# Out-norm of three head groups ahead of the last pages, an LRU gate without reciprocal, and part of the SSD on GpSimd

## The reference

```python
def rms_norm(x, g):
    y = x * lax.rsqrt(jnp.mean(x * x, axis=-1, keepdims=True) + EPS)
    return y * g

# RG-LRU
a = jnp.exp(log_a)
bterm = jnp.sqrt(-jnp.expm1(2.0 * log_a)) * (i * xb)
# SSD, carried states
h = chunk_decay * h + states
# mixer output, heads of 64
y = jnp.concatenate([y_ssd, y_lru, y_hgrn2, y_mla], axis=-1).reshape(b, L, 16, 64)
y = rms_norm(y, out_norm.reshape(16, 64)).reshape(b, L, 1024)
x = x + g2 * (y @ w_out)
```

## Time and profile before

| | |
|---|---|
| runs | 1904.53, 1911.35, 1911.89 us; median 1911.35 |
| profiled execution | 1913.51 us, span 1911.8 us, mean granted clock 0.944 |
| busy (share of the span) | PE 1771.8 (93%), DVE 957.6 (50%), ACT 610.9 (32%), POOL 237.4 (12%) |
| chain that ended last | PE 80%, DVE 14%, ACT 3%, DMA 1% |

### The profile page before, as it was taken

The page is one execution under the profiler, slowest core; times in us unless marked ns, Lnnn a source line. Parts: engine busy times, 40 slices in busy tenths (PEclk is TensorE's granted clock), DMA queues, the critical chain, the costliest instruction groups (busy, mean ns, idle before and its releaser), DMA issues.

```text
span 1911.8 us, 28829 instructions
## 1 busy us (share of the span) xinstructions
PE 1771.8 (93%) x11864; PEld 1524.4 (80%) x11864; DVE 957.6 (50%) x1729; ACT 610.9 (32%) x972; POOL 237.4 (12%) x434
## 2 busy tenths in 40 slices
PE   4999999999989788999989999999998887899998
PEld 3999996667667556999979999967766664699998
DVE  3544432465775644354445444236767745444443
ACT  2433321033231324343334333111433233333331
POOL 8000003510044000000000000072003210000000
PEclk8999999999887889999999999999998788999999
DMA  9566647862011253554453544493201123435542
GB/s 316 192 198 202 207 144 227 272 213 84 1 53 42 101 186 116 166 182 131 162 172 130 178 135 159 149 255 106 93 25 35 38 67 132 132 133 176 169 145 67
DMA packets 206275, 272.06 MB, mean 142 GB/s; under 512 B 11778, under 2 KB 182238, under 8 KB 206144
## 3 DMA queue, kind: packets, MB, share of 16 engines
q1 hardware_dynamic: 188240, 236.90, 37.9%
q0 software_dynamic: 17904, 33.33, 6.1%
...
## 4 chain that ended last, share of the span: by engine, by line
PE 80%; DVE 14%; ACT 3%; DMA 1%; issue 1%; SPq 0%; DVEq 0%; ACTq 0%
PE bank L782 16%; PE bank L784 16%; PE bank L783 16%; PE bank L913 10%; PE bank L1048 4%; PE bank L1309 4%; PE bank L719 2%; DVE sq L2269 2%; PE bank L1221 1%; PE bank L709 1%; DMA ring<-in_w_ada_dram 1%; DVE big L1995 1%; PE bank L1021 1%; PE bank L1191 1%; DVE zs L1628 1%
## 5 line engine op out<-in xcount | busy, mean ns | idle before, releaser
L784 PE MATMUL bank<-hT_r,ring_r 128*128 128x320 f32 x1408 | 440.5, 313 | 0.0
L784 PEld LDWEIGHTS bank<-hT_r,ring_r 128*128 128x128 f32 x1408 | 267.5, 190 | 0.0
L1636 DVE TENSOR_TENSOR ring_r<-ring,lat_pages_r 128x2048 fp32r<-128x2048 f32 (+1 forms) x68 | 151.4, 2229 | 162.4 <-ACT lat_pages_r L1335 162.4
L782 PE MATMUL bank<-hT_r,lat_pages_r 128*128 128x320 f32 x704 | 218.9, 311 | 13.5 <-DVE gates_r L1668 13.5
L783 PE MATMUL bank<-gates_r,lat_pages_r 128*128 128x320 f32 x704 | 219.3, 312 | 0.0
L784 PE MATMUL bank<-big_r,ring_r 128*128 128x320 f32 x704 | 218.0, 310 | 0.0
L913 PE MATMUL bank<-hT,ring 128*128 128x320 f32 x736 | 209.6, 443 | 4.7 <-DVE hT L1662 4.7
L913 PEld LDWEIGHTS bank<-hT,ring 128*128 128x128 f32 x736 | 140.9, 194 | 65.2 <-issue 11.6
L1335 ACT ACTIVATE lat_pages_r<-ring 128x2048 fp32r<-128x2048 f32 (+1 forms) x68 | 126.4, 1862 | 142.8 <-DMA ring<-in_w_ffn_in_dram 69.4
L782 PEld LDWEIGHTS bank<-hT_r,lat_pages_r 128*128 128x128 f32 x704 | 134.0, 190 | 19.0 <-issue 18.5
L783 PEld LDWEIGHTS bank<-gates_r,lat_pages_r 128*128 128x128 f32 x704 | 133.9, 190 | 0.0
...
## 6 DMA issues: line engine op xcount, KB each, us to landing
...
lat_pages<-in_cache_mla_latent_dram POOLq DMA_DIRECT2D x128, 64.0 KB, 2.2
...
```

The lines of the kernel that those rows point to most:

```text
L782: mm(out, w_h, x_h, start=start, stop=False)
L784: return mm(out, w_l, x_h, start=False, stop=stop)
L1636: go(v.tensor_tensor(slot_r(n, nk, 256), slot(n, nk, 256), w_hi_r[g % HI][:, 0:nk].bitcast(F32), ALU.subtract), w_low)
```

## The change

- The sum products of the out-norm go to bank 7 in halves (one chunk each), ScalarE takes the root straight from the bank (scale and epsilon inside it), and VectorE inverts the root and multiplies in one step, `scale`. `invert` and the semaphore `on_inv` go. `BATCH` puts MLA's prompt batch third, and batches 0 to 2 are squared, summed and scaled around `from_states` and `score(5)` instead of after it; batch 3 stands before `soft_exp(2)` on ScalarE and before `soft_values(2)` on VectorE. Dummy products go (14 before `turn(5)`, 20 before `soft_turn(2)`).
- The LRU takes sqrt((1 + a^2) t) in place of sqrt(2 t/(1 + t)): one square on ScalarE, one product on VectorE.
- GpSimd does `spread_b` and the decay of the SSD states, between its page loads. On VectorE `att_inv(0)` and `att_scores(0)` follow `turned_states(1)`; on TensorE `turn(1)` follows `new_states(0)`, with 8 dummy products after it in place of 12.

```diff
-BATCH = [(0, 0, T), (2, 0, T), (4, 0, T), (6, 0, TP), (6, TP, T)]
+BATCH = [(0, 0, T), (2, 0, T), (6, 0, TP), (4, 0, T), (6, TP, T)]
+BATCH_AT = [0, 640, 0, 1280, 640]
...
+        def norm_tmp(n):
+            _, c0, c1 = BATCH[n]
+            return carve(sq, BATCH_AT[n], 2, T)[:, :, c0:c1]
...
     store_latents(pool, l)
+    def spread_b(j):
+        pool.tensor_tensor(bm_blk[0:64], bm_tok[0:64, 2, j * P:(j + 1) * P].unsqueeze(1).to_broadcast([64, NB, P]),
+                           c("seqmask", 64).unsqueeze(2).to_broadcast([64, NB, P]), ALU.mult).then_inc(blk_ready, 1)
+    pool.wait_ge(rest_loaded, 16)
+    pool.wait_ge(ssd_dve, at(ssd_dve, 3))
+    spread_b(0)
+    pool.wait_ge(ssd_act, at(ssd_act, 3))
+    pool.wait_ge(ssd_pe, at(ssd_pe, 4))
+    for j in range(2):
+        ends = Es[:, j, P:].rearrange("p (b t) -> p b t", b=NB)[:, :, TS - 1]
+        pool.tensor_tensor(ssd_state[:, j], ssd_state[:, j], ends.unsqueeze(2).to_broadcast([P, NB, P]),
+                           ALU.mult).then_inc(decayed, 1)
+    pool.wait_ge(ssd_pe, at(ssd_pe, 5))
+    spread_b(1)
     pool.wait_ge(group_used, at(group_used, 1))
...
     keep_busy(8)
-    turn(1)
-    keep_busy(12)
     pe.wait_ge(ssd_dve, at(ssd_dve, 5))
 
     def new_states(j):
 
+        pe.wait_ge(blk_ready, at(blk_ready, j + 1))
         for q in range(2):
             ins = mm(bank[1 + q][:, :], xdt_end[0:64, 2, j * P:(j + 1) * P], bm_blk[0:64, 4 * q:4 * q + 4],
                      start=True, stop=True)
...
     for j in range(2):
         pe.transpose(bank[0][:, j * P:(j + 1) * P], hp[:, j], c("ident"))
     new_states(0).then_inc(ssd_pe, 1)
+    turn(1)
+    keep_busy(8)
     score(1)
...
+    def out_norm(n, half):
+        if half == 0:
+            pe.wait_ge(on_sq, at(on_sq, n + 1))
+        if n or half:
+            pe.wait_ge(on_root, at(on_root, 2 * n + half))
+        _, c0, c1 = BATCH[n]
+        mm(bank[7][:, c0:c1], c("ones64"), norm_tmp(n)[:, half], start=True, stop=True).then_inc(on_pe, 1)
...
     value_taken(1)
     turn(4)
     score(4)
-    keep_busy(14)
+    out_norm(0, 0)
     turn(5)
+    out_norm(0, 1)
     pe.wait_ge(hg_dve, at(hg_dve, 7))
     block_sums(2).then_inc(hg_pe, 1)
+    out_norm(1, 0)
     from_states(0, 0, 0).then_inc(hg_pe, 1)
+    out_norm(1, 1)
     from_states(1, 1, 0)
+    out_norm(2, 0)
     from_states(2, 1, 256).then_inc(hg_pe, 1)
+    out_norm(2, 1)
     score(5)
-    def out_norm(n):
-        pe.wait_ge(on_sq, at(on_sq, n + 1))
-        if n:
-            pe.wait_ge(on_inv, at(on_inv, n))
-        k0, c0, c1 = BATCH[n]
-        for k in range(k0, k0 + 2):
-            ins = mm(bank[2 + k % 2][:, c0:c1], c("ones64"), sqx[:, k, c0:c1], start=True, stop=True)
-        ins.then_inc(on_pe, 1)
 
     tail_tiles, tail_steps = iter(TAIL[l]), sorted({step for step, _ in TAIL[l]})
 
...
         if i < len(tail_steps):
             ada_turn(tail_steps[i])
 
-    keep_busy(20)
     soft_turn(2)
     soft_spread(2)
-    out_norm(0)
+    out_norm(3, 0)
     tail(1)
+    out_norm(3, 1)
     value(2)
     value_taken(2)
     turn(6)
-    out_norm(1)
-    tail(1)
+    tail(2)
     score(6)
     tail(2)
-    out_norm(2)
     turn(7)
     tail_turn(0)
     tail(1)
     score(7)
-    out_norm(3)
     tail(4)
     soft_turn(3)
     tail_turn(1)
...
     tail(1)
     value(3)
     value_taken(3)
+    pe.wait_ge(on_root, at(on_root, 8))
     for h in range(4):
         r = slice(64 * (h % 2), 64 * (h % 2) + 64)
         ins = mm(bank[7][r, (h // 2) * 64:(h // 2) * 64 + 64], wv[:, h * 64:(h + 1) * 64],
                  pn.rearrange("p b (h t) -> p b h t", h=4)[:, :, h], start=True, stop=True)
     ins.then_inc(mla_pe, 1)
     tail(3)
-    out_norm(4)
-    tail(2)
+    out_norm(4, 0)
+    tail(1)
+    out_norm(4, 1)
+    tail(1)
     tail_turn(2)
...
+    def on_square(n):
+        ac.wait_ge(mixed, at(mixed, n + 1))
+        k0, c0, c1 = BATCH[n]
+        if n == 2:
+            ac.wait_ge(on_scaled, at(on_scaled, 1))
+        o.go(f(norm_tmp(n), hT[:, k0:k0 + 2, c0:c1], ACT.Square), on_sq)
+    def on_sqrt(n):
+        _, c0, c1 = BATCH[n]
+        for half in range(2):
+            ac.wait_ge(on_pe, at(on_pe, 2 * n + half + 1))
+            o.go(f(norm_tmp(n)[:, half], bank[7][:, c0:c1], ACT.Sqrt, bias=eps, scale=1.0 / 64), on_root)
...
         o.go(f(la[:, j], lr[:, j], ACT.Exp, scale=lam8[:, j:j + 1]))
-        o.go(f(lt[:, j], lr[:, j], ACT.Tanh, scale=nlam8[:, j:j + 1]), lru_act)
+        o.go(f(lt[:, j], lr[:, j], ACT.Tanh, scale=nlam8[:, j:j + 1]))
+    o.settle()
+    o.go(f(lm, la, ACT.Square), lru_act)
     ac.wait_ge(lru_dve, at(lru_dve, 1))
-    o.go(f(lm, lm, ACT.Sqrt, scale=2.0), lru_act)
+    o.go(f(lm, lm, ACT.Sqrt), lru_act)
     att_copy(2)
     att_squares(2)
     att_root(2)
...
     att_root(3)
     soft_exp(1)
     att_copy(4)
+    on_square(0)
+    on_square(1)
     att_squares(4)
     att_root(4)
+    on_sqrt(0)
     att_copy(5)
+    on_sqrt(1)
+    on_square(2)
+    on_sqrt(2)
     att_squares(5)
     att_root(5)
-    def batch(x, n):
-        k0, c0, c1 = BATCH[n]
-        return x[:, k0:k0 + 2, c0:c1]
-    def on_square(n):
-        ac.wait_ge(mixed, at(mixed, n + 1))
-        o.go(f(batch(sqx, n), batch(hT, n), ACT.Square), on_sq)
-    def on_sqrt(n):
-        ac.wait_ge(on_inv, at(on_inv, n + 1))
-        o.go(f(batch(sqx, n), batch(sqx, n), ACT.Sqrt), on_root)
-    for n in range(4):
-        on_square(n)
+    on_square(3)
+    on_sqrt(3)
     soft_exp(2)
-    on_sqrt(0)
     att_copy(6)
-    on_sqrt(1)
     att_squares(6)
     att_root(6)
     tail_copy(0)
     att_copy(7)
-    on_sqrt(2)
     att_squares(7)
     att_root(7)
     tail_copy(1)
     soft_exp(3)
-    on_sqrt(3)
     on_square(4)
+    on_sqrt(4)
     tail_copy(2)
-    on_sqrt(4)
     tail_copy(3)
...
-    def spread_b(j):
-        go(v.tensor_tensor(bm_blk[0:64], bm_tok[0:64, 2, j * P:(j + 1) * P].unsqueeze(1).to_broadcast([64, NB, P]),
-                           bview(c("seqmask", 64), P), MUL))
-    spread_b(0)
     for cc, (t0, L) in enumerate(TC):
         ve.wait_ge(ssd_act, at(ssd_act, 4 + cc))
         if cc == 2:
...
     turned_states(0)
     o.settle()
-    att_inv(0)
-    att_scores(0)
     ve.wait_ge(ssd_pe, at(ssd_pe, 4))
     do(v.tensor_copy(hp, bank[3][:, 0:256].rearrange("p (j n) -> p j n", j=2)))
     for j in range(2):
         go(v.scalar_tensor_tensor(last_ssd[:, j], hp[:, j], Es[:, j, P - 1:P], bank[3][:, (2 + j) * P:(3 + j) * P], MUL, ADD))
-        ends = Es[:, j, P:].rearrange("p (b t) -> p b t", b=NB)[:, :, TS - 1]
-        go(v.tensor_tensor(ssd_state[:, j], ssd_state[:, j], bview(ends, P), MUL))
     turned_states(1)
     o.settle()
+    att_inv(0)
+    att_scores(0)
     hg_gates()
     ve.wait_ge(ssd_pe, at(ssd_pe, 5))
     go(v.tensor_copy(hpT, bank[0][:, 0:256].rearrange("p (j n) -> p j n", j=2)))
...
             s = ssd_state[:, j, 4 * q:4 * q + 4]
             go(v.tensor_tensor(s, s, bank[1 + q][:, :].rearrange("p (b n) -> p b n", b=4), ADD))
-    spread_b(1)
+    ve.wait_ge(decayed, at(decayed, 2))
     add_states(0)
     o.tell(ssd_dve)
     att_inv(1)
...
     soft_values(0)
-    ve.wait_ge(lru_act, at(lru_act, 2))
-    do(v.tensor_scalar(lm, lt, 1.0, None, ADD))
-    do(v.reciprocal(lm, lm))
-    do(v.tensor_tensor(lm, lm, lt, MUL), lru_dve)
+    ve.wait_ge(lru_act, at(lru_act, 1))
+    do(v.scalar_tensor_tensor(lm, lm, 1.0, lt, ADD, MUL), lru_dve)
...
-    go(v.tensor_tensor(hT[:, 2:4], lh, gelu, MUL))
+    do(v.tensor_tensor(hT[:, 2:4], lh, gelu, MUL))
+    for n in range(3):
+        o.tell(mixed)
     go(v.tensor_tensor(wf, wf, kh, MUL), hg_dve)
...
         w = hg_state[:, :, 4 * i:4 * i + 4]
         go(v.tensor_tensor(w, w, bank[2 + i].rearrange("p (j v b) -> p j b v", j=2, b=4), ADD))
     o.tell(out_ready)
+    def scale(n):
+        k0, c0, c1 = BATCH[n]
+        x = norm_tmp(n)
+        ve.wait_ge(on_root, at(on_root, 2 * n + 2))
+        do(v.reciprocal(x, x))
+        for k in range(k0, k0 + 2):
+            y = hT[:, k, c0:c1]
+            go(v.scalar_tensor_tensor(y, y, col("out_norm", k), x[:, k - k0], MUL, MUL), on_scaled if k > k0 else None)
+    scale(0)
+    scale(1)
     ve.wait_ge(hg_pe, at(hg_pe, 5))
     add_from_states(0, 0, 0)
     ve.wait_ge(hg_pe, at(hg_pe, 6))
...
     add_from_states(2, 1, 256)
     o.settle()
     do(v.tensor_tensor(hT[:, 4:6], oacc, gh, MUL))
-    for n in range(4):
-        o.tell(mixed)
+    o.tell(mixed)
+    scale(2)
     att_inv(5)
     att_scores(5)
     soft_max(2)
-    def invert(n):
-        k0, c0, c1 = BATCH[n]
-        ve.wait_ge(on_pe, at(on_pe, n + 1))
-        for k in range(k0, k0 + 2):
-            go(v.tensor_scalar(sqx[:, k, c0:c1], bank[2 + k % 2][:, c0:c1], 1.0 / 64, EPS, MUL, ADD))
-        o.settle()
-        go(v.reciprocal(sqx[:, k0:k0 + 2, c0:c1], sqx[:, k0:k0 + 2, c0:c1]), on_inv)
-    def scale(n):
-        k0, c0, c1 = BATCH[n]
-        ve.wait_ge(on_root, at(on_root, n + 1))
-        for k in range(k0, k0 + 2):
```

(24 more changed lines are left out.)

2 lines of the change are left out of this document (removed).

## The result

The changed kernel takes 1921.3 us (median of 7 runs, 1915.2 to 1931.5) against 1911.6 for the kernel before: a ratio of 1.0063 with the interval [1.0043, 1.0082], 12 us slower by the ratio, 10 by the medians. I had said "within 0.5%, 1907.3", with a range that ended at 1920. The profiled execution is a good one of its kernel: 1918.1 us, span 1916.4.

A forecast was written before the change was run, and what follows sets the result against it. Bound: mixer stages, by waits behind small steps, above all VectorE reciprocals, with TensorE's clock partly halved. Sum +0.3 - 3.6 + 9.2 - 7.3 - 2.6 = -4.0 us from 1911.35 gives 1907.3, within 0.5%; range 1893 to 1920.

The forecast's parts named there:

- my slower rival: Idling where 14 dummy products stood before turn 5 halves the clock: 5.3 us per layer there, 1923 in all; chance 0.16.
- +0.3: SSD stage, both layers: `score(1)` slightly earlier in layer 0 (-0.3), later in layer 1 (+0.6), GpSimd work free.
- I take 0, and +1 per layer at the upper end: SSD spread and decays on GpSimd: cost nothing on the path unless they outlast their cover.
- my 4.5 of cover: SSD decays on GpSimd: up to 4.5 us for each is hidden before VectorE asks for them.
- `score(1)` at 499.5: SSD stage, layer 0: page 1's scores start at 499.5 against 499.76, after turn 1 and 8 dummy products (1.8 us).
- +9.2 and -9.9: Out-norm, both layers: early sums at `from_states` cost 9.2 us; the tail gains 7.3 and 2.6.
- my 2.5: Tail, without the 20 dummy products before `soft_turn(2)`: TensorE idles, half clock costs 2.5 us a layer (none to 5).
- LRU -3.6: LRU without reciprocal: TensorE's waits before `score(2)`, 1.66 and 1.98 us, disappear; gain 3.6 us for both layers.
- The cap by dummy products: LRU: 28 dummy products (6.36 us) stand before `score(2)`, so anything gained beyond TensorE's remaining wait is hidden.
- From_states 4.6 a layer: Five halves of sum matmuls before `score(5)`: 2.9 us at full clock plus 1.7 for half clock, 4.6 per layer.
- as soon as the 8-column products fill the engine: `from_states`: clock granted at half from 614.1 on, so the last three sum halves double, +1.7 us.
- The tail: From `soft_spread(2)` on: +2.0 first, for roots and a 4.15 us reciprocal, then gains; -9.8 layer 0, -5.1 layer 1, before half-clock loss.

The follow-up runs named there:

- `lru_20`: LRU part alone on the kernel before, with 20 dummy products instead of 28 ahead of `score(2)`: 1907.0 us, ratio 0.9966.
- `no_ssd`: The changed kernel with the SSD part undone, leaving the LRU and out-norm parts: 1910.8 us, ratio 1.0011 to the kernel before.

## Why the prediction was wrong

The number of my slower rival, 1923 for "the wait before turn 5" (0.16 of the chance), is near the 1921.3 measured, but it is near by luck. It priced the SSD part at +0.3 us, and that part alone costs 9.6 by its ratio. It priced the loss from turn 5 on at 5.3 us a layer above my forecast, where the changed kernel's trace has 1.7 and 1.5. What it has right is the kind of loss, a lower clock once the dummy products are gone. Two terms of the sum failed, SSD and out-norm.

- **The SSD part, "+0.3"**, is where the trace itself contradicts the sum. "I take 0, and +1 per layer at the upper end" for GpSimd was wrong by 2.1 us a layer. I asked only whether GpSimd would be done in time. The decays were (1.89 us each, well inside my 4.5 of cover). The damage is the other way round: VectorE's copy waits for a GpSimd product nobody is waiting for yet. I had priced an operation's length and its reader, and not its neighbour on the other engine. With the spreads back on VectorE 4 us return by the ratios.
- **`score(1)` at 499.5** took the turn and 16 records of dummy products at full clock. After 3.71 us of idling the turn ran at half (1.97 us) and so did part or all of the dummy products: turn 1 to the scores took 4.5 us in layer 0 and 5.5 in layer 1 where I had 3.1. With the GpSimd term this is 8 of the 9.6 us that the SSD part costs.
- **The out-norm part, +9.2 and -9.9 = "-0.7"**, holds in the profiled execution (-1.3) and fails in the median (+8.4, by the ratio +10.5). The step that failed is the price of lower clock: the lost dummy products ahead of turn 5 at nothing and those ahead of `soft_turn(2)` at 2.5 us a layer, 5.0 in all. Ten and 20 of them put back give 8.4 by the ratios (4.8 by the medians). Taken out of the kernel before, they cost 11.1 together; alone the first cost 5.0 us a layer and the second 1.0 to 2.0, which its interval doesn't tell from my 2.5. I didn't believe the rival's 5.3 because the trace of before shows no fall at that place. It can't: it shows the clock with the dummy products in front. Where in the changed kernel the 8.4 us are lost stays open.
- **"LRU -3.6"** was right: -3.4 alone. The cap by dummy products was the right way to see it: the scores start with no wait. That more is to be had behind the cap is not shown (`lru_20`).
- **"From_states 4.6 a layer"** was right for the halves (4.6 and 4.9) and low for the stretch: 6.3 and 6.1, by turn 5 in layer 0 and the longer half clock among the 8-column products. That the clock falls "as soon as the 8-column products fill the engine" is not what the rows say. Before, they had run since 609.4 when it fell at 614.1, and in the changed kernel their first 128 records are at full clock in layer 0.
- **The tail**: turn 6 to output projection -13.0 and -6.4, forecast -11.8 and -7.1: right in size. In front of turn 6 the size was right too (+4.8 and +4.3 for 4.5). My 2.5 for half clock has its reason there; the 2.0 for the 4.15 us reciprocal does not. The reciprocal is done in time, and what stands on the path are the roots and their table ahead of the exponential.
- **The base**: I summed against one execution at a clock of 0.944 and carried the difference over to the median. The kernel before usually runs at 0.948 and the changed one at 0.939. A part that lowers the clock isn't seen in a sum of instructions, and hardly in one trace.

The three parts by their ratios add up to +16.7 us, and the whole change costs 12; `no_ssd` is 5 below its two parts too. That gap is not explained.
